# The DeltaNet layer of a decoder trunk: two weight units moved into the opening, weight splits spread over each step

## The reference, cut to what matters

```python
proj = h @ w_in                     # q, k, v, z, beta, a
qkv = silu(causal_conv(proj[..., :GD_QKV], conv_w))      # 4 taps
q = l2norm(q) * GD_DK ** -0.5; k = l2norm(k)             # 8 heads; v and z have 16
a_mat = where(strict, (k k^T) * gamma * beta, 0)         # 64 x 64 chunks
t_mat = inverse(a_mat + eye)
u = t_mat @ (v * beta);  w = t_mat @ (k * beta * exp(G))
# over the chunks, one after the other:
v_new = u - w @ S
o = (q * exp(G)) @ S + (qk * gamma) @ v_new
S = decay * S + k_g^T @ v_new
o = rmsnorm(o) * gain * silu(z)                          # then o @ w_out
```

## Time and profile before

| | us |
|---|---|
| median of 3 runs | 2310.96 (2309.2 to 2312.33) |
| the profiled execution's own time | 2311.65 |
| its span, first to last instruction | 2309.9 |
| mean granted TensorE clock | 0.992 |
| PE busy | 2262.4 (98%) |
| DVE, ACT, POOL busy | 1229.7, 989.4, 368.8 |
| the DeltaNet stage, input part | 1406 to 1852 |

### The profile page before, as it was taken

One profiled execution on the slowest core, in us unless ns is written; L12 is line 12 of the kernel. 1 busy time (PEld: TensorE's weight loads), 2 busy tenths in 40 slices (PEclk: granted clock), 3 DMA queues, 4 the chain that ended last, 5 costly groups with the idle time before them and its releaser, 6 DMA issues.

```text
span 2309.9 us, 32401 instructions
## 1 busy us (share of the span) xinstructions
PE 2262.4 (98%) x11770; PEld 1869.9 (81%) x11770; DVE 1229.7 (53%) x1570; ACT 989.4 (43%) x1445; POOL 368.8 (16%) x295
## 2 busy tenths in 40 slices
PE   9999999899999999999999998999899999999999
PEld 7888888788788888888888886876777888888887
DVE  5445436666465444355454338856666634555423
ACT  5323335655453333344323336466566634332322
POOL 2112100110112111001121001021722100121100
PEclk9999999999999999999999999999999999999999
DMA  5322332222223222323232323222112122433331
GB/s 169 104 91 86 93 94 97 71 79 77 77 74 104 96 91 84 98 92 109 91 100 77 100 87 95 83 66 72 56 46 80 50 93 72 133 104 104 108 134 64
DMA packets 84727, 208.06 MB, mean 90 GB/s; under 512 B 25088, under 2 KB 29312, under 8 KB 84640
## 3 DMA queue, kind: packets, MB, share of 16 engines
q1 hardware_dynamic: 84112, 206.59, 28.5%
q10 hardware_dynamic: 528, 0.26, 0.0%
HBM read 202.56 MB, written 4.26 MB: 90 GB/s over the span
## 4 chain that ended last, share of the span: by engine, by line
PE 87%; DVE 6%; ACT 3%; POOL 2%; issue 1%; DMA 0%; SPq 0%; DVEq 0%; ACTq 0%; POOLq 0%
PE bank L1959 67%; PE bank L2259 8%; PE bank L2041 5%; DVE w_lo L1151 1%; DVE h_lo L1156 1%; POOL gd_o L1872 1%; ACT h_hi L628 1%; POOL sq L1869 1%; ACT w_hi L616 1%; DVE resid L1186 1%; PE bank L2421 1%; PE bank L2400 1%; PE bank L2428 1%; DVE gate L1439 0%; PE bank L2404 0%
## 5 line engine op out<-in xcount | busy, mean ns | idle before, releaser
L1151 DVE TENSOR_TENSOR w_lo<-raw,w_hi 128x1024 fp32r<-128x1024 f32 x395 | 562.4, 1442 | 452.7 <-ACT w_hi L616 452.6
L1959 PE MATMUL bank<-h_hi,w_hi 128*128 128x512 f32 (+1 forms) x1799 | 694.6, 386 | 8.8 <-DVE h_lo L1156 3.5
L1959 PE MATMUL bank<-h_hi,w_lo 128*128 128x512 f32 (+1 forms) x1799 | 683.7, 380 | 0.0
L1959 PE MATMUL bank<-h_lo,w_hi 128*128 128x512 f32 (+1 forms) x1772 | 673.7, 380 | 0.0
L616 ACT ACTIVATE w_hi<-raw 128x1024 fp32r<-128x1024 f32 x395 | 414.7, 1055 | 559.9 <-PE bank L1959 452.7
L1959 PEld LDWEIGHTS bank<-h_hi,w_hi 128*128 128x128 f32 x1799 | 339.1, 188 | 81.1 <-DVE w_lo L1151 7.2
L1959 PEld LDWEIGHTS bank<-h_hi,w_lo 128*128 128x128 f32 x1799 | 338.9, 188 | 64.7
L1959 PEld LDWEIGHTS bank<-h_lo,w_hi 128*128 128x128 f32 x1772 | 334.1, 189 | 64.2 <-issue 2.6
L1799 POOL TENSOR_TENSOR y<-y,up 128x512 f32<-128x512 f32 x88 | 171.4, 1948 | 833.5 <-DVE up L1230 646.9
L1230 DVE TENSOR_TENSOR up<-bank,rms 128x512 f32<-128x512 f32 x88 | 60.7, 690 | 340.2 <-PE bank L1959 340.2
L1959 PE MATMUL bank<-act_hi,w_hi 128*128 128x512 f32 (+1 forms) x594 | 217.6, 366 | 0.0
(11 more groups left out here) (305 smaller groups left out, 2670.5 us busy)
## 6 DMA issues: line engine op xcount, KB each, us to landing
raw<-in_ffn_in SPq DMA_DIRECT2D x172, 512.0 KB, 3.6
raw<-in_gd_in SPq DMA_DIRECT2D x49, 512.0 KB, 3.6
raw<-in_ffn_out SPq DMA_DIRECT2D x48, 384.0 KB, 3.1
raw<-in_hg_in SPq DMA_DIRECT2D x32, 512.0 KB, 3.4
raw<-in_ffn_out SPq DMA_DIRECT2D x48, 320.0 KB, 2.9
raw<-in_last_out SPq DMA_DIRECT2D x22, 512.0 KB, 3.5
raw<-in_gd_out SPq DMA_DIRECT2D x16, 512.0 KB, 3.6
raw<-in_hg_out SPq DMA_DIRECT2D x8, 512.0 KB, 3.4
```

The source lines that it names most:

```text
L1151: nc.vector.tensor_tensor(w_lo[:, r, :], raw[:, r, :], w_hi[:, r, :].bitcast(f32), ALU.subtract).then_inc(lo_split, 1)
L1959: ins = nc.tensor.matmul(dst[:, half(h)], w, moving[ml][:, k, :][:, half(h)], start=first and n == 0 and (wl, ml) == (0, 0), stop=last and ...
```

## The change

Four things are rewritten; the arithmetic, the number of units and the instructions are the same but for one: the silu over six early gate rows (`early_silu`) is cut in three.

1. Opening, PE: units 6 and 7 run whole after `key_sum(0)` and `key_sum(1)`; all later work is moved one unit on. Banks and waits follow: unit 7 goes to bank 2, so that `key_blocks(0)` waits until the value rows of unit 7 are drained (`drained` 8, before 3).
2. Opening, DVE and ACT: `value_drain(0, 1)` ahead of `key_norm(2)`, the columns of `substitute` parcelled otherwise, two gate silus and two weight splits moved into step 1.
3. Steps: weight splits are spread (`n0+2` and `n0+3` inside the chain of the chunks, `n0+4` behind `value_drain`), only one or two remain in the tail; `out_gate` is moved to the next step; `from_lanes(1, ...)` goes behind the query convolution; `to_lanes(1)` is cut in two, its second half (`to_lanes_scaled`) being in step 3.
4. Step tails, PE: two pieces are kept for after `level_u6`, and both `value_transpose` stand behind the other pieces. ACT: `evict_u6` after the tail's splits.

```diff
-            return {4: 7, 8: 6, 9: 7}[n] if n in (4, 8, 9) else n % 2
+            return {4: 7, 7: 2, 8: 1, 9: 7}[n] if n in (4, 7, 8, 9) else n % 2
...
# ACT, step(j)
-                    part_of(n0 + 3)
                     new_value(g, 0)
+                    part_of(n0 + 2)
                     if g == 0:
-                        key_tap(5)
-                        key_silu(4)
+                        gate_silu_out(0, 0)
+                        gate_silu_out(0, 1)
                     elif g == 1:
                         key_tap(7)
-                        key_silu(6)
+                        early_silu(2, 4)
                     else:
                         gate_silu_out(g - 1, 1)
                     new_value(g, 1)
+                    if g == 0:
+                        key_tap(5)
+                    if g < 2:
+                        key_silu(2 * g + 4)
                     decays(j, 0)
+                    if g > 1:
+                        part_of(n0 + 3)
+                    new_value(g, 2)
+                    if g < 2:
+                        key_silu(2 * g + 5)
+                    decays(j, 1)
+                    query_tap(j)
+                    if g < 2:
+                        part_of(n0 + 3)
                     if g == 1:
-                        key_silu(7)
-                    new_value(g, 2)
-                    decays(j, 1)
-                    if g == 0:
-                        key_silu(5)
-                    query_tap(j)
+                        early_silu(4, AHEAD)
                     part_of(n0 + 4)
                     keys_by_token(j)
                     new_value(g, 3)
...
+                    value_tap(j, 1)
                     value_silu(j, 0)
-                    part_of(n0 + 5)
-                    value_tap(j, 1)
+                    evict_p6(j)
+                    value_silu(j, 1)
                     values_by_token(j, 0)
-                    evict_p6(j)
-                    part_of(n0 + 6)
-                    value_silu(j, 1)
                     values_by_token(j, 1)
+                    for n in range(n0 + 5, q_unit(j + 1) + 2):
+                        part_of(n)
                     evict_u6(j)
-                    for n in range(n0 + 7, q_unit(j + 1) + 3):
-                        part_of(n)
...
# DVE, step(j)
+                    memory(g, 0)
+                    if g == 0:
+                        lo(n0 + 2)
+                    elif g == 1:
+                        key(6, (1,))
+                    elif g == 2:
+                        to_lanes_scaled(1)
+                    else:
+                        lo(n0 + 2)
+                    residual(g, 1)
...
+                        out_gate(g - 1, 0)
+                    value_decay(g, 1)
...
+                        out_gate(g - 1, 1)
+                    memory(g, 1)
...
+                    elif g < 3:
+                        lo(n0 + 2)
+                    else:
+                        lo(n0 + 3)
+                    residual(g, 2)
...
+                    query(j)
+                    if g < 3:
+                        lo(n0 + 3)
                     if j == 4:
                         from_lanes(1, 1)
...
                         from_lanes(1, 0)
-                    value_decay(g, 2)
...
+                    value_drain(j, 0)
                     lo(n0 + 4)
-                    query(j, (2, 3))
-                    value_drain(j, 0)
                     out_norm(g)
...
# DVE, opening
                 query(0)
                 value_drain(0, 0)
+                value_drain(0, 1)
                 key_norm(2)
                 key_norm(3)
                 lo(9)
                 to_lanes(0)
...
# PE, waits of the opening
-                        if n in (8, 9):
-                            pe.wait_ge(k_logged, n - 5)
+                        if n == 9:
+                            pe.wait_ge(k_logged, 4)
...
                     if i == 0:
-                        pe.wait_ge(drained, 3)
+                        pe.wait_ge(drained, 8)
...
# PE, tail of step(j)
                         scores(j)
-                        piece(4)
-                        value_transpose(j, 0)
+                        piece(4 if j == 1 else 2)
                         level_p6(j)
...
-                        piece(4)
+                        piece(len(todo) - 2)
+                        value_transpose(j, 0)
                         value_transpose(j, 1)
                         level_u6(j)
                     piece(len(todo))
...
# PE, opening
                 key_sum(0)
+                unit(6, whole)
+                key_sum(1)
...
-                key_sum(1)
-                unit(6, whole[:3])
+                unit(7, whole)
                 key_sum(2)
-                unit(6, whole[3:])
                 key_sum(3)
-                unit(7, whole[:2])
+                unit(8, whole[:2])
                 key_blocks(0)
                 key_blocks(1)
```

More of the change, by code:

```diff
@@ L1000, in step @@
                     new_value(g, 3)
-                    query_silu(j)
-                    out_square(g)
+                    if g < 2:
+                        out_square(g)
+                        query_silu(j)
+                    else:
+                        query_silu(j)
+                        out_square(g)
                     query_square(j)
@@ L1562, in step @@
                     if g == 0:
-                        key(4, (1, 2))
-                        memory(g, 0)
                         key(4, (3,))
+                    elif g == 1:
+                        key_drain(7)
+                    else:
+                        gate_out(g - 1, 1)
+                    memory(g, 0)
+                    if g == 0:
+                        lo(n0 + 2)
+                    elif g == 1:
+                        key(6, (1,))
+                    elif g == 2:
+                        to_lanes_scaled(1)
+                    else:
+                        lo(n0 + 2)
@@ L1566, in step @@
+                    residual(g, 1)
+                    if g == 0:
                         key_drain(5)
                     elif g == 1:
-                        key_drain(7)
-                        memory(g, 0)
-                        key(6)
-                    else:
-                        gate_out(g - 1, 1)
-                        memory(g, 0)
-                    lo(n0 + 3)
-                    residual(g, 1)
+                        key(6, (2,))
+                    else:
+                        out_gate(g - 1, 0)
@@ new lines, in step @@
+                    value_decay(g, 1)
+                    if g == 1:
+                        key(6, (3,))
+                    elif g > 1:
+                        out_gate(g - 1, 1)
+                    memory(g, 1)
+                    if g == 0:
+                        key(5, (1,))
+                    elif g < 3:
+                        lo(n0 + 2)
+                    else:
+                        lo(n0 + 3)
+                    residual(g, 2)
+                    if g < 2:
+                        key(2 * g + 5, (1,) if g else (2,))
@@ new lines, in step @@
+                    value_decay(g, 2)
+                    if g < 2:
+                        key(2 * g + 5, (2,) if g else (3,))
+                    else:
+                        query_drain(j)
+                    memory(g, 2)
+                    if g == 0:
+                        query_drain(j)
+                    elif g == 1:
+                        key(7, (3,))
+                    residual(g, 3)
+                    if g == 1:
+                        query_drain(j)
+                    query(j)
@@ L1588, in step @@
-                    residual(g, 2)
-                    if j == 4:
-                        from_lanes(1, 0)
-                    value_decay(g, 2)
-                    if g == 1:
-                        key(7, (3,))
-                    query_drain(j)
-                    memory(g, 2)
-                    residual(g, 3)
-                    query(j, (1,))
+                        from_lanes(1, 0)
+                    value_drain(j, 0)
                     lo(n0 + 4)
-                    query(j, (2, 3))
@@ L1635, in last_step @@
                     memory(g, 0)
+                    lo(n0 + 2)
+                    residual(g, 1)
+                    out_gate(g - 1, 0)
+                    value_decay(g, 1)
+                    out_gate(g - 1, 1)
+                    memory(g, 1)
                     lo(n0 + 3)
-                    residual(g, 1)
-                    out_gate(g - 1, 1)
-                    value_decay(g, 1)
+                    residual(g, 2)
                     head_low(0)
-                    memory(g, 1)
-                    head_low(1)
-                    residual(g, 2)
-                    head_low(2)
-                    head_low(3)
                     value_decay(g, 2)
@@ L1648, in last_step @@
                     memory(g, 2)
-                    head_low(4)
+                    head_low(1)
```

(11 more changed lines are left out.)

100 lines of the change are left out of this document (44 added, 56 removed).

## The result

The changed kernel takes 2288.76 us (median of 4 runs, 2288.34 to 2290.6), the kernel before 2310.4 us beside it: ratio 0.9908, 95% interval [0.9896, 0.992], so 21.6 us faster. 2286 us had been forecast, a gain of 25.1. Its profiled execution has a span of 2286.6 us (before 2309.9) at a mean granted clock of 0.995 (before 0.992).

A forecast was written before the change was run, and what follows sets the result against it. PE is busy 98% of the span, so only its waits and slow clock can give time. 9.8 + 2.0 + 1.5 + 8.3 + 5.2 = 26.8 us, less 1.7 of clock, 25.1: from 2310.96 to 2286 us, range 2278 to 2300.

The forecast's parts named there:

- case A: Whole stage: the gains come as summed, 2286 us, own range 2278 to 2294; chance 0.60.
- Opening: Stage's opening: units 6 and 7 cover PE's waits and lost clock, 11.4 less 1.6 of new waits, 9.8 us gained.
- Rival B: Opening: DVE becomes the bound and about half the gain there is lost, 2291 us; chance 0.15.
- Step 1: Residual wait and 1.5 us before the second value transpose go, a 0.5 us wait for `evict_u6` comes; 2.0 us gained.
- Step 2: Old waits of 4.5 us go, new ones of 3.0 come, 2.2 of them at `attend(1, 3)`; 1.5 us gained.
- Tails, steps 5 to 7: Three tails lose 1.3 us of waits each, less 0.45, plus 1.7 of clock in step 7; 5.2 us gained.
- Steps 3 and 4: DVE's wait for POOL's last column goes, POOL's later start costs 4.0 us; 84.0 instead of 92.3, 8.3 us gained.
- The clock: Behind new waits in step 2 (2.2 us) and step 4 (2.7 us): one loss of 1.7 us taken.
- Rival C: POOL's inversion stretches beside a denser DVE, 20% on 42.7 us, felt at `attend(3, 0)`; 2294.5 us, chance 0.10.
- D: Every step: waits move from DVE to ACT's queue, 2 to 3 us each, no net change, 2309 us; chance 0.07.
- E: Splits inside the chunk chain: late ACT halves cost waits and clock in seven steps, slower, 2314.5 us; chance 0.08.

The follow-up runs named there:

- e7: Changed kernel with PE's old order in the opening alone, units 6 and 7 behind the first key sums as before; 2295.85 us.
- e10: Changed kernel with DVE's `decayed_keys(0)` in the opening put behind 2.7 us of its own later work; 2289.45 us.
- e3: Changed kernel with the split `lo(n0 + 3)` of steps 4 to 7 moved from ahead of `residual(g, 2)` to behind `query(j)`; 2290.25 us.
- e6: Changed kernel with PE's old order in the tails of steps 3 to 7 alone, no pieces behind `level_u6`; 2295.13 us.
- e1: Changed kernel with `to_lanes_scaled(1)` moved from step 3 back to the tail of step 2, directly behind `to_lanes(1)`; 2282.67 us.
- e5: Changed kernel with step 4's two `from_lanes` transposes back at their old places, behind the residuals; 2298.04 us.
- e9: Changed kernel with the edits of e1, e2 and e3, plus step 2's split `part_of(n0 + 3)` ahead of `new_value(1, 2)`; 2279.17 us.
- e2: Changed kernel with `early_silu(4, AHEAD)` moved from step 2's `new_value` chain to behind `evict_u6`; 2287.64 us.
- e8: Kernel before with one part of the change alone: step 4's two `from_lanes` transposes behind the query convolution; 2301.13 us.
- e11: e9 with the opening's `key_blocks` in a row behind four pieces of unit 8 instead of two and two; 2277.82 us.

## Why the prediction was right, and where it was off

The time came out 2.8 us above the forecast, inside case A's own range (2278 to 2294). The gain was 21.6 us of the 25.1 forecast. By the steps of the sum:

- **Opening, 9.8 forecast, 9.7 measured.** No wait for the table, no fall of the clock near 1428. The profile of the changed kernel stands 1.0 us earlier than that of the kernel before (its stage begins at 1407.5, before 1408.5); with that added, the drain ended at 1443.0 (forecast 1443.1), PE was there at 1441.4 (forecast 1441.8), and the first `new_values` came at 1506.4 (forecast 1506.5). `key_blocks(0)` waited 1.6 us where 1.3 was forecast. One reading was wrong: the longest of nine waits for a silu, 1.5 us, lies in step 1, and the one at the end of the opening was 1.3. So that term was 0.2 too large, and that the sum came within 0.1 is in part luck. e7, which undoes PE's new order around the key sums, costs 6.3 of the 9.7 us. The other 3.4 are the silu wait and the slow stretch behind it, both gone from the trace; no run undoes that part alone. Rival B fell: `decayed_keys` ended before PE came, and e10 found 1.3 us in hand (forecast 0.8).
- **Step 1, 2.0 forecast, 2.6 measured.** The wait of 0.5 us for `evict_u6(1)` did not come: ACT's copy, behind its two splits, ended as PE got there, and PE was busy for all of the step.
- **Step 2, -0.2 with the clock, -0.5 measured.** The new waits were found where they were put: `attend(1, 3)` 2.1 us (forecast 2.2, though the forecast's own 20.0 - 17.5 gives 2.5), the first decay 0.5 as forecast, and the value transpose of the tail 0.9 (forecast 0.3). The fall of the clock behind the first of them came: 3.4 us at half, 1.7 lost.
- **Tails, steps 5 to 7, 5.2 forecast, 4.3 measured.** The term mis-sized was the tax of `lo(n0 + 3)` ahead of `residual(g, 2)`: 0.15 a step in the sum, 0.3 by e3. The tails themselves gave 1.0 a step in e6, plus the silu wait that it leaves out; 1.3 had been taken.
- **Steps 3 and 4, 8.3 forecast, 6.2 measured. The largest miss.** The mechanism was right: POOL, started later by DVE's scaling, is what PE waits for. The premise that failed is that POOL keeps its pace. It started 2.7 us later (forecast 2.9), but its columns took 1.4 us longer, the copies for `half_6` 0.9 and those for `inv_t` 0.4. So `half_6` was 5.0 us late, and PE, which would have waited some 0.3 us for it at `level_p5(3)` with POOL at its old pace, waited 2.6; and `level_t5(3)` started 3.9 us later than in e1, where 1.3 had been charged. `masked_probs(3)` ended as forecast (46.6, forecast 46.8) only because POOL's later instructions were faster, above all the queries. That agreement was luck, and of no use: PE was late itself by then, and `attend(3, 0)`, charged with 2.7 us, did not wait. 3.9 us at one place where 4.0 had been charged at two, so in the sum this error cancelled. What did not cancel is the slow clock behind it, 1.7 us from `level_t5(3)` to the end of step 3 (12.7 us there, 11.0 in e1), and 0.3 in step 4 for `lo(n0 + 3)`. e1 shows the size of it all: without the late start the pair takes 80.8 us. No run holds POOL's start where it is and gives it back its pace, so the two parts of the delay are told apart by the rows alone.
- **The clock.** One loss of 1.7 us was taken for two new waits, and each had one: 1.7 in step 2, 1.7 in step 3. The evidence for taking one was misread: the slow stretch at the end of the opening follows a wait of 1.3 us, and the wait of 1.5 us in step 1 has none behind it. Step 7 shows a fall behind waits of 0.3 and 0.7 us (last section), so the length of a wait was no ground for choosing.

Rival C was put as a longer queue, 20% on 42.7 us, and fell in that form: the queue took 42.6. In its first part, which decides, it came true at 10% (29.0 us for 26.3). D and E fell: the chunk chain lost 0.3 us a step (e3), not 2 or more, and no wait of steps 4 to 7 stands in PE's list. The moves of splits and silus on DVE and ACT inside the steps were not undone as a whole in any run; what they gave beside e3, e5 and e6 is argued from the waits that went.

The Trainium skill (TensorE: Matmul & The Clock Gate, "Why this matters for your kernels") asks that gaps stay under about 3 us. This case's traces disagree: a wait of 2.1 us was followed by 3.4 us at half clock, and one of 2.6 by 6.8. By that rule the forecast would have been 1.7 us lower and the miss larger.

## What to carry to other kernels

When a step is moved, list everything that waits for its engine's *next* engine, in the order in which TensorE wants it, and find the time of each hand-over. The length of the whole queue is not enough: GpSimd's kept its 42.7 us, while the part up to the first hand-overs grew from 26.3 to 29.0, and TensorE waited there. A scaling of 1.2 us on VectorE, moved from the end of one step into the next, reached TensorE by way of GpSimd and cost 5 to 6 us, a quarter of what the whole change gained. A wait taken away in a queue with slack behind it pays; in a step in which another engine is as late, it moves to the next semaphore (e9), so before you spend the edit look at what the wait would end with if this one came in time. And cover a wait with pieces of independent work rather than by making the producer faster: two pieces of 0.9 us at each place gave 1.0 us a tail and 1.9 us in the opening, with no instruction added.

## What the runs showed of the hardware

**The price of one and the same wait is not fixed.** In step 2 of the changed kernel and of e1, e3, e5, e6 and e7 the wait at `attend(1, 3)` is 2.1 us and the step 48.9 us long, with the clock down. In e10, where the code of that step is the same and only the opening is 1.4 us longer, the same wait of 2.1 us stands in PE's list, and the step takes 47.3. The changed kernel's slow stretch, and the same place of e10:

```profile
1573.90:1577.30 3.40, 3.40 (x11) 2.77 (x10) 2.12 (x2) 3.09 (x5) 0.43 (x1) 0.51 0.16 25
```

```profile
1573.00:1583.00 10.00, 7.92 (x32) 5.29 (x31) 8.29 (x8) 9.52 (x17) 3.71 (x3) 1.00 0.17 55
```

0.51 is the level of 1.2 GHz, 1.00 that of 2.4. TensorE's instructions ahead of the wait are the same in both. Step 3 varies likewise: behind the same wait of 2.6 us at `level_p5(3)` the clock was down for 6.8 us in five profiles (changed kernel, e2, e6, e7, e10) and for some 10.1 in two (e3, e5), whose code is that of the changed kernel up to there. The step took 45.7 us in the changed kernel and e10 and 47.2 in e3 and e5. (46.0 in e7 and 46.6 in e2 have another wait, 0.5 and 1.2 us, for `inv_t`; the 46.7 of e6 has 1.0 of its own edit.) The stretch in e3:

```profile
1633.60:1643.70 10.10, 10.10 (x101) 7.88 (x101) 4.33 (x7) 5.56 (x9) 9.39 (x12) 0.50 0.01 2
```

Nor does the length of a wait decide. In the kernel before, each of the steps 5, 6, 7 and 8 begins behind a wait of 0.3 us for a silu and, 2 us later, one of 0.7 for `inv_t`. The clock stays at 1.00 around the start of steps 5, 6 and 8, and falls at that of step 7, in e8 as well:

```profile
1788.00:1795.00 7.00, 6.32 (x36) 5.32 (x34) 3.16 (x8) 2.99 (x6) 0.00 (x0) 0.76 0.29 94
```

A wait of 1.3 us at the end of the opening was followed by 3.4 us at half clock, one of 1.5 us in step 1 by none, both in the kernel before and in e8; the five waits of 1.0 us in e6 by none. What decides it stays open: no run here moved a wait by small steps. So a wait is to be priced at its own length and a possible loss of clock, here 1.7 us behind the one in step 2 and 1.7 to 3.1 between `level_t5(3)` and the end of step 3. It also means that a single profile can't tell a gain of 1 us in a kernel that has such a wait; e9 and e11, in whose stage the clock never fell, are the better ground for small edits.

**GpSimd slows by place, not evenly.** The two copies for `half_6` took 1.48 us in the kernel before, 1.50 in e1, and 2.36 in the changed kernel, and 2.35 or 2.36 in all six other profiles that have them at that place (e2, e3, e5, e6, e7, e10). In the changed kernel VectorE ran three convolution taps beside them, from 1628.53 to 1632.03; in the kernel before it was idle until 1639.09, for all but the last 0.2 us of them. No run varies this alone, so that the taps are the cause is not shown. The first sixteen columns, with the same elements, took 22.2 us before, 23.6 in the changed kernel and 24.4 in e1.
